# Routed experts: the gather of the third tile ahead is issued before the scatter of the tile behind

## The reference, cut to what matters

```
for every block of 128 (token, expert) pairs, experts in rising order:
    x    = h2[tok]                                # gather 128 rows of 1024
    y    = (silu(x @ w1[e]) * (x @ w3[e])) @ w2[e]
    sum[tok] += y * gate[:, None]                 # scatter with an addition
shared = (silu(h2 @ ws1) * (h2 @ ws3)) @ ws2      # the same, every token, in order
x = x + g2 * (routed + shared)
```

## Time and profile before

| | us |
|---|---|
| median of 3 runs (2837.97 to 2843.45) | 2840.59 |
| the profiled execution | 2836.76 |
| its span | 2835.0 |
| first gather issued | 1339.9 |
| last scatter issued | 2776.6 |
| PE busy in the span | 2541.6 (90%) |
| POOL busy in the span | 991.8 (35%) |

### The profile page before, as it was taken

How to read it: one execution, slowest core, us unless ns; L and a number is a source line. 1 busy time by engine, 2 the same in 40 slices (tenths; PEclk the granted TensorE clock), 3 DMA queues, 4 the chain that set the end, 5 groups by cost and what they waited for, 6 DMA issues and landing times. The chain is left out here.

```text
span 2835.0 us, 51166 instructions
## 1 busy us (share of the span) xinstructions
PE 2541.6 (90%) x11957; PEld 2031.0 (72%) x11958; DVE 1733.6 (61%) x2714; ACT 1014.7 (36%) x1615; POOL 991.8 (35%) x1006
## 2 busy tenths in 40 slices
PE   7999999999849889669999999999998999999990
PEld 4787777777638777558777777777776788777780
DVE  4664564574236666664775775775589745686643
ACT  3212444323212222132442453543356422454422
POOL 1210035602245665521233433433333333343334
PEclk9999999999969998889999999999999999999995
DMA  7865768574456555255897887997789966698757
GB/s 276 312 256 200 266 229 307 198 277 163 163 211 227 167 167 167 86 162 124 280 291 207 238 258 222 292 276 212 193 262 356 301 186 155 165 341 267 211 107 270
DMA packets 239095, 641.38 MB, mean 226 GB/s; under 512 B 24108, under 2 KB 37744, under 8 KB 223536
## 3 DMA queue, kind: packets, MB, share of 16 engines
q1 hardware_dynamic: 188736, 459.72, 45.4%
q0 software_dynamic: 50288, 180.75, 26.0%
HBM read 463.06 MB, written 177.33 MB: 226 GB/s over the span
## 5 line engine op out<-in xcount | busy, mean ns | idle before, releaser
L2043 POOL DMA_INDIRECT sum_d<-w_shared_raw,give x136 | 235.7, 1733 | 786.6 <-DVE w_shared_raw L2185 560.2
L2143 DVE TENSOR_TENSOR w_exp_lo<-w_exp,w_exp_hi (+1 forms) x256 | 307.5, 1221 | 86.2 <-ACT w_exp_hi L2082 68.8
L2289 PE MATMUL ps_h<-w_exp_hi,x_exp_t_hi 128*128 (+1 forms) x1216 | 315.2, 402 | 31.6 <-ACT w_exp_hi L2082 25.8
L2082 ACT ACTIVATE w_exp_hi<-w_exp (+1 forms) x256 | 260.8, 1056 | 191.6 <-DMA w_exp<-in_experts 106.6
L2289 PE MATMUL ps_h<-w_exp_hi,x_exp_t_lo 128*128 (+1 forms) x1216 | 321.7, 406 | 0.0
L2289 PE MATMUL ps_h<-w_exp_lo,x_exp_t_hi 128*128 (+1 forms) x1216 | 311.1, 398 | 0.0
L2289 PEld LDWEIGHTS ps_h<-w_exp_hi,x_exp_t_hi 128*128 128x128 f32 x1216 | 229.2, 190 | 93.8 <-ACT w_exp_hi L2082 21.3
L1134 PE MATMUL ps_p<-wa_hi,hx_split 128*128 128x512 f32 x1088 | 278.0, 401 | 4.3 <-DVE kvqg_out L100 3.3
L2289 PEld LDWEIGHTS ps_h<-w_exp_lo,x_exp_t_hi 128*128 128x128 f32 x1216 | 230.3, 189 | 56.5
L2108 ACT ACTIVATE h_exp_t_hi<-ps_ht 128x256 fp32r<-128x256 f32 x152 | 58.1, 383 | 531.3 <-PE ps_ht L2298 510.7
L2289 PEld LDWEIGHTS ps_h<-w_exp_hi,x_exp_t_lo 128*128 128x128 f32 x1216 | 217.7, 189 | 41.4
(11 more groups left out here) (276 smaller groups left out, 4396.4 us busy)
## 6 DMA issues: line engine op xcount, KB each, us to landing
w_exp<-in_experts SPq DMA_DIRECT2D x386, 512.0 KB
hx_split<-hx_d SPq DMA_DIRECT2D x54, 1024.0 KB, 6.0
rec_m<-rec_d SPq DMA_DIRECT2D x16, 1536.0 KB, 7.5
hx_d<-hx_split SPq DMA_DIRECT2D x18, 1024.0 KB, 7.0
wm_rest<-in_w_mod_rest POOLq DMA_DIRECT2D x16, 1024.0 KB, 6.1
rec_d<-kvqg_out SPq DMA_DIRECT2D x48, 256.0 KB, 4.2
xt<-in_xt POOLq DMA_DIRECT2D x18, 512.0 KB, 8.8
rec_d<-kt_kvf_out SPq DMA_DIRECT2D x32, 256.0 KB, 4.9
```

Of the source, the lines that this page charges most:

```text
L2043: pool.indirect_dma_start(sum_d[:, :], bass.IndirectOffsetOnAxis(give[:, par:par + 1], 0), y[:, par], None, compute_op=ALU.add).then_inc(a ...
L2082: act.activation(w[0][:, piece(e, i)].bitcast(F32R), raw(e, i), ACT.Copy).then_inc(gu_hi, 1)
L2143: dve.tensor_tensor(w[1][:, piece(e, i)].bitcast(F32R), raw(e, i), w[0][:, piece(e, i)], ALU.subtract).then_inc(gu_lo, 1)
L2289: last = pe.matmul(out, x[:, j * P:(j + 1) * P].bitcast(F32R), w_part[:, bass.ds(w_at + j * stride, 512)].bitcast(F32R), start=(start and ...
```

## The change

The step of POOL gathers one tile further ahead. In step k it now issues the gather of tile k+3, then the scatter of tile k-1. One gather, of tile 18, is written out ahead of the steps. Nothing else moves: the waits inside `gather` and `scatter` are the same functions of the tile's number, so the gather of tile k+3 waits for the transposes of tile k+1, which PE does in its own step k ahead of `down(k - 1)`. The buffers are the same two. One gather more is issued in all (139), and the last wait counts it.

```
             for k in range(11, NT - 1):
                 add(k)
 
+            gather(NT + 2, 0, 1)
+
             def step(k, par, r):
-                gather(k + 2, par, r + 1)
+                gather(k + 3, 1 - par, r + 1 + par)
                 if isinstance(k, int) and k == NT:
                     add(NT - 1)
                 else:
...
-            pool.wait_ge(gathered[0], (n + 1) * 16)
+            pool.wait_ge(gathered[0], (n + 2) * 16)
             pool.wait_ge(gathered[1], (n + 1) * 16)
```

## The result

| | before | changed |
|---|---|---|
| median, us | 2840.53 (2837.97 to 2843.45, 4 runs) | 2800.18 (2798.24 to 2807.26, 4 runs) |
| profiled execution, us | 2836.76 | 2798.24 |
| its span, us | 2835.0 | 2796.4 |
| first to last matmul of the transposes, us | 1367.7 to 2763.9: 1396.2 | 1366.0 to 2724.8: 1358.8 |
| PE idle in the routed tiles, us | 77.8 of 1440 | 49.9 of 1401 |

The ratio is 0.9862, with a 95% interval of 0.9842 to 0.9882: faster by 40 us. The forecast was 2812, with a range of 2802 to 2829. Between the two profiled executions, 37.4 of the 38.6 us of span fall between the first and the last of the transposes, and 1.7 us lie ahead of them, where the two kernels are the same; the tail is 0.5 us longer.

What follows compares the result with a forecast made beforehand. PE, busy 90% of the span, was taken as the bound, with at most 77.8 us to win in the routed tiles. -31.0 + 5.4 - 6.2 + 3 = -28.8, say -29, from 2840.6: 2812 us, range 2802 to 2829.

Steps and rivals of the forecast that it cites:

- The gather's lead: PE's transposes: gathers asked for about 16 us ahead, so all 20 waits for gathered rows go, -31.0 us.
- What is late next: PE's `down` still waits for the low half of the hidden values at some of the 20 places, +5.4 us.
- The refill: PE's slower start after a wait costs 0.39 us at each of 16 places; winning it back gives -6.2 us.
- Weights: Experts come sooner, so weight pieces come late and part of the gain is lost: +3 us, between 0 and 12.
- The scatter and the extra gather: POOL's queue: the gather ahead of the scatter and one more gather at the end cost 0, up to 5 for the latter.
- rival C: Scatters behind gathers land up to 2.4 us later and their chain becomes the bound: 2903, or 2857 at half; chance 0.05.

Runs made afterwards that it cites:

- e8: The changed kernel unchanged, run again beside the kernel before on the same chip: 2802.9 us, ratio 0.9853.
- e2: The changed kernel, but only gathers of even tiles go out early, those of odd tiles stay behind the scatter: 2830.1 us, ratio 0.9955 to the kernel before.
- e3: The changed kernel, but only gathers of odd tiles go out early, those of even tiles stay behind the scatter: 2837.2 us, ratio 0.9980 to the kernel before.
- e12: The kernel before, unchanged, run once more for a second trace: 2816.5 us in one run.
- e6: The changed kernel with each routed tile's scatter replaced by a write of 64 bytes a row: 2781.0 us, ratio 0.9776 to the kernel before.
- e5: The kernel before with each routed tile's scatter replaced by a write of 64 bytes a row: 2782.0 us, ratio 0.9784.
- e9: The kernel before, but from the fifth expert on each weight piece moves a quarter of its bytes: 2763.4 us, ratio 0.9808.
- e11: The kernel before with the gather of tile k+2 issued after the scatter of tile k-1: 3912.7 us in one run.
- e1: The changed kernel, but the gather of tile k+3 also waits until tile k-1 is weighed: 2816.3 us, ratio 0.9909 to the kernel before.

## Why the prediction was right in its mechanism and short in its size

1. *The gather's lead: right.* I wrote 31.0 us of waits gone. All went. The lead at the tile of the earlier trace rows is 16.7 us (forecast about 16); in undisturbed tiles the gather goes out 1.2 us after the transposes end and 4.0 us ahead of the scatter (2020.16, 2021.39 and 2025.41 in the last rows of the timeline above).

2. *What is late next: right.* Forecast +5.4 us and a wait of about 37 us; measured 37.6, and 37.9 in e8. In the 20 tiles that had waited, PE's wait for the hidden values rose from 1.4 to 5.9 us, as the prediction had it.

3. *The refill: the step that failed.* The prediction put what a wait costs beside its idle time at 0.39 us in the tile behind it, at 16 places, -6.2 us; with the waits that makes -37.2. I compared tile by tile. The 20 tiles with a wait became 33.0 us shorter, though 4.5 us of the wait for hidden values came into them, so they had lost more than their 31.0 us of idle time. The 18 tiles that follow one of them and had no wait themselves became 4.3 us shorter, 0.24 us each and not 0.39. What was missing stands in the waits of the weight loads, a view I had read past:

```profile
PEld ps_x L2283 <- issue: 42.7, 30, 3.0
```

The weight loads of the transposes were held 42.7 us at 30 places, where the matmuls show 31.0 us at 20: the end of the matmul before is modelled and covers the start of a wait. Of the 42.7 us, 39.6 lie at the same 20 places, 0.43 us more at each, and only 3.1 at ten places where the matmuls show nothing. The same hidden part is the busy time that fell by 11.0 us; so the idle time of 77.8 us, which the prediction took as the most that can be won, was no upper bound. One of the ten short ones, of before:

```profile
1839.29 0.86 PEld L2283 LDWEIGHTS ps_x<-ident,w_shared_raw 128*128 128x128 f32 x8 [0.36 <-issue]
1839.30 1.09 PE L2283 MATMUL ps_x<-ident,w_shared_raw 128*128 128x128 f32 x8
```

The eight matmuls take 1.09 us, the mark of a start after a wait, and none is recorded. The changed kernel has no such row. The simple account is -42.7 + 5.4 = -37.3 us, and the stage fell by 37.4. It holds for e2 within a us: 33.8 us on the weight loads, and a wait for the hidden values 8.8 us below the changed kernel's, make 25.0; its stage is 24.3 longer. It does not always hold so well. For e3, 32.9 - 1.7 = 31.2 falls short of 37.0, and a lower clock does not tell e3 from e2: both have a granted clock of 0.99 over the stage, the changed kernel 1.00. From e12 to e8, -40.7 + 6.9 = -33.8, while the stage fell by 38.4. So the agreement to 0.1 us is in part luck; the account is good to some 6 us, and what the rest is stays open.

4. *Weights: wrong.* I took +3 us, up to 12, and no row stood behind it. ACT's wait named weights fell by 10.5 us (93.4 to 92.7 between e12 and e8), but its wait that the profile names "issue" rose from 84.6 to 99.1, so the fall may be one of names. What counts is PE: its wait for the split weights was 4.7 us and is 3.6. The stretch at a DMA share of 0.90 went to 0.94, and nothing of it shows on PE.

5. *The scatter and the extra gather: right at 0, though in part from wrong rows.* The landing times that rival C was worked out from were misread. The earlier trace rows is over all transfers that touch `sum_d`, and in the traces before and after it holds no routed scatter: their landings are not told there, and the 7.6 and the 15.1 us are of plain transfers ahead of and behind the experts. So 6.7 us in the changed kernel and 7.2 in e8 say nothing on the scatters either. The landing of the routed scatters is told in e12, by its line 2043:

```profile
DMA to landing us min/median/max: 5.9/6.5/11.2
```

C was still less likely by these, with 11.2 and not 15.1 us as the longest against the 16.9 at hand, and it did not show: POOL's waits for landings rose from 209.3 to 245.1 us (194.1 in e12, 232.9 in e8), but DVE's fell from 14.5 to 6.8, and PE lost nothing. Whether each gather was through when the scatter came, some 4 us later, no trace of the changed kernel tells; in e6 gathers took 4.4 us in the median and up to 8.2, so not all were. The queue's ring order did not hurt all the same. At the end, the last scatter went out at 2737.3, 39.3 us sooner than before (2776.6), so the extra gather cost nothing.

So two terms of the sum were mis-sized: waits and refill by 5.5 us, weights by 3. With the weights at 0 and 42.7 in place of 31.0 + 6.2, the sum would have been -37 and the forecast 2803. The remaining 3 us between that and 2800.2 are of the size by which the part ahead of the routed tiles differs (it ends at 1366.0 in this trace, at 1369.6 in e8's). The range was too narrow below: it ended at 39 us of gain, and its own terms had no entry for waits not seen.

## What to carry to other kernels

If a transfer has two buffers and its rows are read one stage before the rest of the tile is done, ask for the next rows as soon as the buffer's last reader is through, ahead of any instruction on that queue which waits for a later result; an instruction that waits is a wall for all behind it. Read a PE wait from the rows of the weight loads as well as from the matmuls, and use the larger; it gave the gain of the stage to within some 6 us. Do not share out a total of waits over single tiles: they cover for each other, and half of the cure gave a third of the gain or less.

## What the runs showed of the hardware

A gather of 512 KB took up to 10.1 us from issue to use when it was moved beside a scatter with addition and weights. Without the scatter's data it landed in 4.6 us in the median and 8.8 at most (e5), with a quarter of the weight bytes in 5.0 and 8.3 (e9), and was in time in all tiles but one. A scatter with addition of 512 KB landed in 6.5 us in the median, 11.2 at most (e12). TensorE starts a group after a short wait slower (1.09 us for eight transposes, not 1.03). With a wait in every tile, 6.5 us in the mean, its granted clock was 0.78 over the stage, and each wait cost 2.2 us beside its idle time (e11). DVE's split waited up to 3.9 us when POOL's copy and gather came directly behind the weighing (e1).
